# The moving columns of a matmul read in runs of 16, in turns from the two halves of a block

## The reference, cut to what matters

```python
x = x + 0.5 * swiglu_ffn(rms_norm(x, g1), w_gate, w_up, w_down)      # 2048 -> 5632 -> 2048
u = rms_norm(x, g2) @ w_in                                           # 2048 -> 9536, split in six
y_conv = layer_norm_silu(depthwise31(a * sigmoid(gate))) @ w_pw_out  # 2048 -> 2048
y_mla = attention(latents of u) @ w_o                                # 16 heads
x = x + (sigmoid(gl_conv) * y_conv + sigmoid(gl_mla) * y_mla) @ w_out
x = x + 0.5 * swiglu_ffn(rms_norm(x, g3), w_gate, w_up, w_down)
return rms_norm(x, final_g)
```

## Time and profile before

| | us |
|---|---|
| median of three runs | 2326.87 |
| the profiled execution | 2326.71 |
| its span, first to last instruction | 2324.8 |
| TensorE busy with matmuls | 2299.0 (99%), 10718 matmuls |
| stationary loads (PEld, beside the matmuls) | 1924.4 (83%) |
| VectorE busy | 1322.2 (57%) |
| ScalarE busy | 1188.3 (51%) |
| the 16 DMA engines | 60% |
| read from HBM | 428.78 MB |

### The profile page before, as it was taken

How to read it: one execution, slowest core, us unless ns; L and a number is a source line. 1 busy time by engine, 2 the same in 40 slices (tenths; PEclk the granted TensorE clock), 3 DMA queues, 4 the chain that set the end, 5 groups by cost and what they waited for, 6 DMA issues and landing times.

```text
span 2324.8 us, 26788 instructions
## 1 busy us (share of the span) xinstructions
PE 2299.0 (99%) x10718; PEld 1924.4 (83%) x10718; DVE 1322.2 (57%) x1470; ACT 1188.3 (51%) x1620; POOL 0.2 (0%) x4
## 2 busy tenths in 40 slices
PE   8999999999999999999999999999999999999997
PEld 7888888888888888878889888888888888888886
DVE  5544544544545488997875465555544544544443
ACT  6444444444444577787776564444444444444443
POOL 0000000000000000000000000000000000000000
PEclk9999999999999999999999999999999999999999
DMA  8666666666665665566643455656666666666664
GB/s 289 189 190 190 190 185 196 190 187 192 190 191 187 186 199 183 171 198 182 199 136 119 138 174 185 189 184 208 188 186 196 191 186 189 191 188 193 195 191 135
DMA packets 121532, 432.65 MB, mean 186 GB/s; under 512 B 13632, under 2 KB 13888, under 8 KB 121280
## 3 DMA queue, kind: packets, MB, share of 16 engines
q1 hardware_dynamic: 121408, 430.93, 60.0%
HBM read 428.78 MB, written 2.10 MB: 185 GB/s over the span
## 4 chain that ended last, share of the span: by engine, by line
PE 97%; DVE 1%; ACT 1%; issue 1%; DMA 0%; SPq 0%; ACTq 0%; DVEq 0%
PE bank L682 31%; PE bank L684 31%; PE bank L683 31%; PE turned L693 2%; PE bank L825 1%; PE bank L799 1%; PE bank L800 1%; DVE q_rope L1117 0%; PE turned L810 0%; ACT w_hi L432 0%; DVE w_lo L927 0%; DVE q_rope L1123 0%; DMA raw<-in_ffn_up 0%; PE turned L879 0%; ACT q_rope L540 0%
## 5 line engine op out<-in xcount | busy, mean ns | idle before, releaser
L927 DVE TENSOR_TENSOR w_lo<-raw,w_hi 128x1024 fp32r<-128x1024 f32 (+2 forms) x814 | 986.9, 1215 | 954.8 <-ACT w_hi L432 954.5
L432 ACT ACTIVATE w_hi<-raw 128x1024 fp32r<-128x1024 f32 (+2 forms) x814 | 853.0, 1051 | 998.4 <-PE bank L684 987.9
L682 PE MATMUL bank<-w_hi,h 128*128 128x512 f32 (+1 forms) x2144 | 835.9, 390 | 10.1 <-DVE w_lo L927 10.1
L684 PE MATMUL bank<-w_hi,h 128*128 128x512 f32 (+1 forms) x2144 | 832.7, 388 | 0.0
L683 PE MATMUL bank<-w_lo,h 128*128 128x512 f32 (+1 forms) x2144 | 832.6, 388 | 0.0
L682 PEld LDWEIGHTS bank<-w_hi,h 128*128 128x128 f32 x2144 | 403.0, 188 | 92.7 <-DVE w_lo L927 11.4
L684 PEld LDWEIGHTS bank<-w_hi,h 128*128 128x128 f32 x2144 | 402.9, 188 | 83.1
L683 PEld LDWEIGHTS bank<-w_lo,h 128*128 128x128 f32 x2144 | 403.1, 188 | 81.6
L682 PE MATMUL bank<-w_hi,hidden 128*128 128x512 f32 x704 | 274.3, 390 | 0.0
L684 PE MATMUL bank<-w_hi,hidden 128*128 128x512 f32 x704 | 273.9, 389 | 0.0
L683 PE MATMUL bank<-w_lo,hidden 128*128 128x512 f32 x704 | 273.9, 389 | 0.0
(11 more groups left out here) (171 smaller groups left out, 1223.4 us busy)
## 6 DMA issues: line engine op xcount, KB each, us to landing
raw<-in_ffn_up SPq DMA_DIRECT2D x352, 512.0 KB, 4.1
raw<-in_ffn_down SPq DMA_DIRECT2D x176, 512.0 KB, 3.6
raw<-in_conv_in SPq DMA_DIRECT2D x64, 512.0 KB, 3.8
raw<-in_conv_gate SPq DMA_DIRECT2D x32, 512.0 KB, 4.2
raw<-in_mla_gate SPq DMA_DIRECT2D x32, 512.0 KB, 4.2
raw<-in_mla_out SPq DMA_DIRECT2D x32, 512.0 KB, 3.6
raw<-in_conv_out SPq DMA_DIRECT2D x32, 512.0 KB, 3.7
raw<-in_w_out SPq DMA_DIRECT2D x32, 512.0 KB, 3.6
```

What stands on the lines that cost most here:

```text
L432: act.activation(w_hi[:, j, 0:n], raw[:, j, 0:n], ACT.Copy).then_inc(hi_ready, 1)
L682: pe.matmul(dst, fixed_hi, moving_hi, start=first, stop=False)
L684: return pe.matmul(dst, fixed_lo, moving_hi, start=False, stop=last)
L927: dve.tensor_tensor(w_lo[:, j, 0:n], raw[:, j, 0:n], w_hi[:, j, 0:n], ALU.subtract).then_inc(lo_ready, 1)
```

## The change

On the host, the columns of a block are cut into runs of 16; the even runs go into the first half of the block's row and the odd ones into the second. In the kernel the moving operand is read with a pattern of three dimensions (run, half, column in the run), so that the columns come in their old order. It reads upwards through both halves. Size, place and number of all buffers, transfers and instructions stay as they were. The empty lines of the diff are left out.

```diff
+RUN = 16
...
+            def in_turns(block):
+
+                return block.rearrange("p (h n t) -> p n h t", h=2, t=RUN)
+
             def wide_unit(u, g):
...
-                    moving = w_hi[:, slot, r * w:(r + 1) * w], w_lo[:, slot, r * w:(r + 1) * w]
+                    moving = in_turns(w_hi[:, slot, r * w:(r + 1) * w]), in_turns(w_lo[:, slot, r * w:(r + 1) * w])
...
 def units_of(w):
     k, width = w.shape
+    w = w.reshape(k, width // (2 * RUN), 2, RUN).transpose(0, 2, 1, 3)
     return w.reshape(k // (DEEP * P), DEEP, P, width).transpose(0, 2, 1, 3).reshape(-1, P, DEEP * width)
```

## The result

The changed kernel takes 2447.49 us (median of four, 2447.18 to 2447.89) where the kernel before takes 2327.10 in the same runs: 1.0519 times as long, 95% interval 1.0502 to 1.0535. That is 120 us slower. Its profiled execution took 2447.18 us.

What follows compares the result with a forecast made beforehand. TensorE was taken to bound the kernel, through 9288 wide matmuls at 226.7 ns a step. The four parts summed as 0 + 0 + 0 + 0 to 2326.9 us, with a range of 2312 to 2450 us.

Steps and rivals of the forecast that it cites:

- rival 1: Moving operand's address walk in wide matmuls: each jump costs a column slot, 12.9 ns a matmul, 2448 us; chance 0.12.
- (a): DMA: one 512 KB transfer per unit, same shape, from a host array of the same size; cost 0.
- (b): Rounding and splitting read and write whole contiguous rows as before, and the head stage is not touched; cost 0.
- Part (c): Moving pattern of 9288 + 96 matmuls, 31 jumps in each wide one: 0, 121 or 241 us; taken as 0.
- second sign: 320-column matmul group: if each jump costs a column slot, proportionally less extra time there, 8 ns.
- Part (d): Moving stream beside the load of the next stationary block: between -97 and +46 us; taken as 0.
- rival 2: Moving stream and stationary load meet for good: step 232 ns wherever a load runs beside, 2373 us; chance 0.14.
- Rival 3: Fixed part of the wide matmul step shrinks: small form 2316 us, chance 0.07; whole form 2230 us, chance 0.05.

Runs made afterwards that it cites:

- moved_flat: The kernel before, contiguous moving operands, with w_hi, w_lo, x and h moved 32 bytes up, hidden and the rest unmoved: 2344.29 us, ratio 1.0075.
- sweep of patterns: In five stages the matmuls read 52 different moving patterns, output not the layer's; one execution, contiguous steps at 227 ns, runs of 16 at 240.
- run64: The changed kernel with runs of 64 in place of 16, the 320-column group keeping 16: 2326.91 us, ratio 0.9999 to the kernel before.
- run32: The changed kernel with runs of 32 in place of 16, the 320-column group keeping 16: 2416.68 us, ratio 1.0385 to the kernel before.

## Why the prediction was right or wrong

The forecast, no change with 0.57, was wrong. The range reached 2450 and held the time, by 2.5 us. That was luck: it did so only because rival 1 was let in, and rival 1's price was right by accident, as shown below.

**What bounds the kernel** was read rightly: TensorE alone, 9288 steps, 9.3 us for each nanosecond. The step rose by 13.1 ns on average and the time by 120 us, with nothing to cushion it. So were (a) and (b): transfers, rounding, splitting and the head stage kept their rows.

**Part (c) is the step that failed**, the price of a jump, in its choice of 0; what the runs show in its place is 13.1 ns a matmul. I took 0 from VectorE's rows, and read them wrongly. L1023 reads all 512 numbers of the PSUM bank in their order, though it names them as eight times 64. What goes back is the other operand, a row of 64 numbers of `trig` that is read eight times:

```python
dve.tensor_tensor(cosines, src, cos[:, None, :].to_broadcast((P, 8, ROPE)), ...)
```

So the row holds 7 breaks in runs of 64 of one operand of two, and for 7 breaks in runs of 64 TensorE too takes 0. The step to 31 breaks in runs of 16 had no row at all, and that is where the price lies. Besides, VectorE spends over 1 ns on an element there and TensorE 0.417 on a column, so that reader may have had time to spare. No run here gives VectorE runs of 16. The plain float32 matmuls show what time can be worth: at two slots a column TensorE walks runs of 16 for nothing (592 ns with and without). I had named the counter-argument myself, that the column rate has no slack, and priced it at 0.12. With no row of a stream without slack, it should have stood above the nearest row of another engine. The remark that a run's 6.7 ns suffice to find the next address rested on nothing; 7.5 passed.

**Rival 1** gave 2448 us, 0.5 us from the result, and its sign in the profile, 240 ns at every wide matmul and at the last one too, came true. Its mechanism did not. It priced each jump at one slot of 0.417 ns; 31 of these are 12.9 ns. The rule that fits the widths is 0.83 ns for each of 32 runs of 16, 26.7 ns, of which the fixed part takes up 13.3. That both come to 13 is chance. Its own second sign showed it, the narrow group with 4.5 ns where it said 8, and runs of 64, where it would say 28 us and got none, settled it; so does the 256-column form, where 15 jumps cost nothing.

**Part (d) and rival 2** were wrong about the changed kernel and right to suspect something in the old one. The step of the change's runs of 16 doesn't hang on the load: the load's width, the base, the distance and the move of 32 bytes all leave 240.0. The load itself took 2 ns longer (190 ns in place of 188). For contiguous reads I concluded from equal medians on h, hidden and merged that addresses don't matter. By the sizes of the buffers, each laid at a multiple of 32 bytes, these operands all stand at the same distance from w_hi modulo 64 numbers, so the rows could not tell. The experiment moved_flat could: 2344 us. The 232 ns behind transposes, which I took as the price of a meeting, appears again, within 4 ns, as the step of contiguous reads off their place, or between jumping ones.

**Rival 3**: the fixed part can shrink, to 3 ns, where the stream reads the same 12 or fewer numbers again and again. No product of this kernel does. With that pattern the trace, at columns + 3.3 ns, comes near the 2.5 ns that the Trainium skill gives in "TensorE: Matmul & The Clock Gate", section "Wait — 56ns, not 53.3ns?"; contiguous fp32r numbers that are read once take columns + 13.3.

Two statements of the Trainium skill, "SBUF — State Buffer", can be held against the runs. Its section "Specifications (TRN2)" wants two hits per line of 16 bytes for full bandwidth. Runs of 16 aligned numbers hit each line four times and lose 6%, and every other number, two hits a line, doubled the step (452 ns in place of 227 in the sweep of patterns). Its section "Who interferes with whom" gives TensorE independent reads for moving operand and load; moved_flat shows a difference of 6 ns a matmul by their distance alone.

**What stays open.** The source of the price is shown: how the moving operand is walked, in a dense stream at one column a slot. Its mechanism is not. No run tells why an upward run of 16 takes 7.5 ns, why the same runs downwards or in falling order take less, why 32 is dearer by the run but not 64, and why runs of 12, 24 and 48 are cheaper than 14, 28 and 72. Three paces describe the data: the column rate with some 3 ns, for 12 or fewer numbers read again and again; the column rate with 13.3 ns, which contiguous reads and runs of 64 and 128 keep at the right distance; and a slower pace for the rest. That is a description and not a cause.

## What to carry to other kernels

Where TensorE streams fp32r at one column a slot, keep the moving operand contiguous, or in runs of 64 or 128 numbers, with every run at a multiple of 64 numbers from its place beside the stationary operand; 64 was free here to within 0.1%, 32 cost 3.9%, 16 cost 5.2%. At 256 columns runs of 16 are free as well (runs of 8 and 4 cost 3 and 7 ns), and in plain float32 so is everything tried. Before the cost of an access pattern is taken from another row, ask which operand it walks in runs, of what length, and whether that engine reads at the limit: a price can hide where there is slack.

## What was not expected of the hardware

A contiguous stream has a place. With the moving operand 4, 8, 16, 32 or 48 numbers off its distance to the stationary one, the mean step is 229 to 233 ns in place of 226.7; 64, 128 and 256 off, and with both shifted by 16, it is 227 again. With both shifted by 4 it is not (232), and with the stationary one alone shifted by 16 it is 233 where the moving one alone gave 229, so distance is not all of it. Moving the weight buffers, x and h by 32 bytes cost the kernel before 17.5 us. For 256 columns it is the other way about (group of L684 on c_kv, c_kv unmoved: 279 ns where the earlier trace rows has 0.28 and the kernel before 283), so short streams gain some 3 ns where long ones lose 6.

Off their place the steps also run in cycles of their own that don't follow the three products: 226, 229, 232 at an offset of 16, 228, 234, 235, 230 at an offset of 4, 235 and 245 in turns for 16 numbers of every 32. Each seems to hand the next its state. The narrow group with runs of 16 shows it best: its instructions are the same in the changed kernel and in run64 and run32, yet it steps at 151 ns in the one and 153 in the others, behind groups with other runs. That is why a mean over a group says more there than a single matmul.
